# Prompt stick attention: f32r sums of a split softplus carried in PSUM, bias and mask added by TensorE, two query chains interleaved, limit and rounding on GpSimd

## What is computed

```python
def stick_breaking(q, k, v, q_pos, k_pos, bias):
    z = jnp.einsum('bqhd,bkhd->bhqk', q, k).astype(jnp.float32) * (q.shape[-1] ** -0.5)
    z = z + bias.astype(jnp.float32)[None, :, None, None]
    mask = k_pos[None, :] < q_pos[:, None]
    log_beta = jax.nn.log_sigmoid(z)
    log_keep = jnp.where(mask, jax.nn.log_sigmoid(-z), 0.0)
    suffix = lax.cumsum(log_keep, axis=3, reverse=True)
    after = jnp.concatenate([suffix[..., 1:], jnp.zeros_like(suffix[..., :1])], axis=-1)
    att = jnp.where(mask, jnp.exp(log_beta + after), 0.0)
    return jnp.einsum('bhqk,bkhd->bqhd', att.astype(v.dtype), v)
```

## Time and profile before

| | |
|---|---|
| median of 3 runs | 1787.25 us (1784.97 to 1789.44) |
| profiled execution, its own time | 1785.31 us |
| its span | 1783.5 us |
| TensorE busy in the span | 1488.5 us, 83% |
| VectorE, ScalarE, GpSimd busy | 649.3, 502.0, 170.1 us |
| prompt stick attention | from 344.6 to 460.5 us of the span, 115.9 us |

### The profile page before, as it was taken

How to read it: one execution, slowest core, us unless ns; L and a number is a source line. 1 busy time by engine, 2 the same in 40 slices (tenths; PEclk the granted TensorE clock), 3 DMA queues, 4 the chain that set the end, 5 groups by cost and what they waited for, 6 DMA issues and landing times. The chain is left out here.

```text
span 1783.5 us, 24367 instructions
## 1 busy us (share of the span) xinstructions
PE 1488.5 (83%) x9557; PEld 1034.4 (58%) x9558; DVE 649.3 (36%) x1011; ACT 502.0 (28%) x1050; POOL 170.1 (10%) x162
## 2 busy tenths in 40 slices
PE   5998997799857888698789989699639999999910
PEld 2446997555636777486349967478324444544400
DVE  4325352387212344567011023275341111111158
ACT  1114233387354343311011134221101111111122
POOL 0000000034102311000000000000011000000046
PEclk9998999699757999899889999899859999999965
DMA  8111110220003000300521044210546776622154
GB/s 296 53 53 30 47 48 24 65 65 1 1 2 111 14 3 3 120 1 1 214 92 48 2 188 166 108 42 1 232 171 226 304 301 229 234 94 94 71 190 148
DMA packets 78750, 182.59 MB, mean 102 GB/s; under 512 B 12692, under 2 KB 40475, under 8 KB 72243
## 3 DMA queue, kind: packets, MB, share of 16 engines
q1 hardware_dynamic: 66891, 137.74, 21.7%
q0 software_dynamic: 7008, 25.43, 4.0%
q10 hardware_dynamic: 4752, 18.02, 2.5%
HBM read 146.40 MB, written 34.86 MB: 102 GB/s over the span
## 5 line engine op out<-in xcount | busy, mean ns | idle before, releaser
L2882 PE MATMUL bank<-arena,hT 128*128 x512 | 232.7, 598 | 2.2 <-DVE hT L2989 2.2
L2882 PEld LDWEIGHTS bank<-arena,hT 128*128 128x128 f32 x512 | 95.9, 192 | 110.9 <-issue 110.9
L2902 PE MATMUL bank<-arena,hT 128*128 x256 | 115.3, 593 | 1.6 <-ACT hT L2940 1.6
L463 PE MATMUL bank<-arena,hT 128*128 128x512 f32 x256 | 112.8, 599 | 0.0
L2016 PE MATMUL bank<-hT_rest,f_w_high 128*128 128x352 f32 x288 | 93.4, 324 | 0.0
L2985 DVE TENSOR_TENSOR hT<-bank,hT 128x256 f32<-128x256 f32 x32 | 13.6, 425 | 216.8 <-ACT hT L2946 216.8
L2852 POOL DMA_INDIRECT hT<-tokens,row_token x32 | 34.2, 1067 | 603.4 <-PE bank L2868 307.2
L463 PEld LDWEIGHTS bank<-arena,hT 128*128 128x128 f32 x256 | 48.7, 193 | 58.4 <-issue 58.3
L2902 PEld LDWEIGHTS bank<-arena,hT 128*128 128x128 f32 x256 | 46.3, 191 | 48.2 <-issue 48.2
L2015 PE MATMUL bank<-hT_high,q_w_high 128*128 128x352 f32 x192 | 62.7, 327 | 7.8 <-DVE q_w_low L2335 7.8
L2015 PE MATMUL bank<-f_h_high_a,f_w_high 128*128 128x352 f32 x180 | 59.0, 328 | 6.7 <-DVE f_w_low L673 6.7
(11 more groups left out here) (463 smaller groups left out, 2955.6 us busy)
## 6 DMA issues: line engine op xcount, KB each, us to landing
arena<-in_ex_wg_dram SPq DMA_DIRECT2D x16, 1024.0 KB, 5.9
arena<-in_ex_wu_dram SPq DMA_DIRECT2D x16, 1024.0 KB, 8.8
arena<-in_ex_wd_dram SPq DMA_DIRECT2D x16, 1024.0 KB, 10.8
expert_rows<-hT ACTq DMA_DIRECT2D x32, 512.0 KB, 2.7
arena<-in_cache_mem_k_dram SPq DMA_DIRECT2D x8, 1024.0 KB, 4.9
arena<-in_w_in_dram SPq DMA_DIRECT2D x12, 512.0 KB, 4.0
h<-in_x_prompt_dram SPq DMA_DIRECT2D x8, 512.0 KB, 8.7
arena<-in_w_in_dram SPq DMA_DIRECT2D x2, 2048.0 KB, 16.7
```

The lines of the kernel that those rows point to most:

```text
L463: last = nc.tensor.matmul(ps[bank][0:r, 0:n], hT[:, k, i * P:i * P + r], wt[:, k, col:col + n], start=(k == 0), stop=(k == KC - 1))
L2882: last = nc.tensor.matmul(ps[UPB[u % 2]][:, :], xT[:, u % 2, k, :], gate_up_of[:, bass.ds(slot, 1), :, k, :].rearrange("p a g f -> p (a g) ...
L2902: last = nc.tensor.matmul(ps[DNB[q]][:, :], hidT[:, u % 2, f, :], down_of[:, bass.ds(slot, 1), f, q * 512:(q + 1) * 512].rearrange("p a n ...
```

## The change

All of it is in `stage_stick_prompt`.

- **Order.** The steps come from two chains of 18, query blocks 7, 4, 3, 0 and 6, 5, 2, 1, one step of either in turn. `first(n)` is a diagonal step, `final(n)` the last key block of a query block.
- **Bias and mask.** The bias is built once as an f32r tile (its rounded part in some rows, the rest of it in others, set by `sel`), and TensorE adds it to the scores by two f32r products with a matrix of ones; on the diagonal two more products add -1e30 where a key is hidden. ScalarE copies the finished scores from PSUM (`evacuate`).
- **Softplus.** GpSimd limits z to 30 (`cut`), ScalarE takes Exp and Ln(1 + x), VectorE the maximum with z. GpSimd rounds the result to f32r (`round_up`), VectorE forms the remainder, also f32r.
- **Sums.** A suffix is two f32r products, the triangle times the rounded part and times the remainder. The sum of earlier blocks stays in the PSUM bank of the chain: once the argument has been read, `rest` adds the other triangle (without the diagonal) times both parts, so that the bank holds the whole blocks.
- Rings grow: five `zb`, three `t`, three each of rounded parts and remainders. Four constant matrices are copied to f32r by ScalarE at the start, and the mask by VectorE.

The diff, cut to its core:

```diff
+    chains = [[(qb, kb) for qb in x for kb in range(qb, -1, -1)] for x in ((7, 4, 3, 0), (6, 5, 2, 1))]
+    steps = [x for two in zip(*chains) for x in two]
+    first = lambda n: steps[n][0] == steps[n][1]
+    final = lambda n: steps[n][1] == 0
+    carried = lambda n: sum(not final(m) for m in range(n + 1))
...
         @block.gpsimd
+            def cut(n):
+                pool.wait_ge(zb_ok, n + 1)
+                if n >= 3:
+                    pool.wait_ge(low_ok, n - 2)
+                nc.gpsimd.tensor_scalar(tmp[:, n % 3], zb[:, n % 5], 30.0, None, ALU.min).then_inc(cut_ok, 1)
+
+            def round_up(n):
+                pool.wait_ge(sp_ok, n + 1)
+                if n >= 3:
+                    pool.wait_ge(sums, n - 2)
+                    pool.wait_ge(carry, carried(n - 3))
+                nc.gpsimd.tensor_copy(high4[:, n % 3], tmp[:, n % 3]).then_inc(high_ok, 1)
+
+            for n in range(N + 2):
+                if n < N:
+                    cut(n)
+                if n >= 2:
+                    round_up(n - 2)
...
         @block.tensor
             def scores(n):
...
+                if n == 0:
+                    pe.wait_ge(consts_ok, 6)
+                    pe.wait_ge(bias_ok, 1)
+                for half in range(2):
+                    q = slice(half * DH, (half + 1) * DH)
+                    last = nc.tensor.matmul(ps[2 * (n % 2) + half][:, 0:256], one[q, :], bias[q, half * 256:(half + 1) * 256],
+                                            start=False, stop=not first(n), skip_group_check=True)
+                if first(n):
+                    for half in range(2):
+                        last = nc.tensor.matmul(ps[2 * (n % 2) + half][:, 0:256], eye, hide,
+                                                start=False, stop=True, skip_group_check=True)
                 last.then_inc(score, 1)
 
             def suffix(n):
                 if n >= 2:
                     pe.wait_ge(arg_ok, n - 1)
+                pe.wait_ge(high_ok, n + 1)
+                nc.tensor.matmul(ps[4 + n % 2][:, :], negsuf, high[:, n % 3 * W:(n % 3 + 1) * W],
+                                 start=first(n), stop=False, skip_group_check=True)
+                pe.wait_ge(low_ok, n + 1)
+                nc.tensor.matmul(ps[4 + n % 2][:, :], negsuf, low[:, n % 3 * W:(n % 3 + 1) * W],
+                                 start=False, stop=True, skip_group_check=True).then_inc(sums, 1)
+
+            def rest(n):
+                if final(n):
+                    return
+                pe.wait_ge(arg_ok, n + 1)
+                nc.tensor.matmul(ps[4 + n % 2][:, :], negbef, high[:, n % 3 * W:(n % 3 + 1) * W],
+                                 start=False, stop=False, skip_group_check=True)
+                nc.tensor.matmul(ps[4 + n % 2][:, :], negbef, low[:, n % 3 * W:(n % 3 + 1) * W],
+                                 start=False, stop=True, skip_group_check=True).then_inc(carry, 1)
...
+            for n in range(N + 5):
+                if n < N:
+                    scores(n)
+                if n >= 5:
+                    values(n - 5)
+                if 4 <= n < N + 4:
+                    rest(n - 4)
+                if 2 <= n < N + 2:
+                    suffix(n - 2)
...
         @block.scalar
+            def evacuate(n):
+                act.wait_ge(score, n + 1)
+                if n >= 5:
+                    act.wait_ge(exp_ok, n - 4)
+                nc.scalar.copy(by_pair(zb[:, n % 5]), score_banks(n)).then_inc(zb_ok, 1)
 
             def softplus(n):
+                act.wait_ge(cut_ok, n + 1)
+                t = tmp[:, n % 3]
+                link(nc.scalar.activation(t, t, ACT.Exp))
                 nc.scalar.activation(t, t, ACT.Ln, bias=1.0).then_inc(soft, 1)
...
+            for n in range(N + 4):
                 if n < N:
+                    evacuate(n)
+                if 1 <= n <= N:
+                    softplus(n - 1)
+                if n >= 4:
+                    weights(n - 4)
...
         @block.vector
+            link(nc.vector.tensor_copy(hi, z0))
+            link(nc.vector.tensor_tensor(z1, z0, hi.bitcast(F32), ALU.subtract))
+            link(nc.vector.tensor_scalar(z0, hi.bitcast(F32), sel[:, 0:1], None, ALU.mult))
+            nc.vector.scalar_tensor_tensor(bias4, z1, sel[:, 1:2], z0, ALU.mult, ALU.add).then_inc(bias_ok, 1)
 
             def soft_sum(n):
                 dve.wait_ge(soft, n + 1)
+                nc.vector.tensor_tensor(tmp[:, n % 3], zb[:, n % 5], tmp[:, n % 3], ALU.max).then_inc(sp_ok, 1)
+
+            def remainder(n):
+                dve.wait_ge(sp_ok, n + 1)
+                dve.wait_ge(high_ok, n + 1)
                 if n >= 3:
                     dve.wait_ge(sums, n - 2)
+                    dve.wait_ge(carry, carried(n - 3))
+                nc.vector.tensor_tensor(low4[:, n % 3], tmp[:, n % 3], high4[:, n % 3].bitcast(F32), ALU.subtract).then_inc(low_ok, 1)
 
             def argument(n):
                 dve.wait_ge(sums, n + 1)
+                nc.vector.tensor_tensor(zb[:, n % 5], head4(4 + n % 2), zb[:, n % 5], ALU.add).then_inc(arg_ok, 1)
...
             for n in range(N + 4):
+                if n < N:
+                    soft_sum(n)
+                if 2 <= n < N + 2:
+                    argument(n - 2)
+                if n < N:
+                    remainder(n)
+                if n >= 4 and final(n - 4):
+                    outputs(n - 4)
```

More of the change, by code:

```diff
@@ L890, in stage_stick_prompt @@
     nc, K = c.nc, c.K
[L891 to L899, removed]
+    W = HEADS * P
+    c.place(start=c.after_q, zb=5 * W, t=3 * W, high=3 * W, low=3 * W, att=2 * W, negsuf=P, negbef=P, eye=P, one=P,
+            bias=W, hide=2 * P)
@@ new lines, in ring @@
+    def ring(x, n):
+        return x.rearrange("p (s h q) -> p s h q", s=n, h=HEADS)
+    zb, tmp, att = ring(c.A("zb"), 5), ring(c.A("t"), 3), ring(c.A("att"), 2)
+    high, low = c.rounded("a_high", "high"), c.rounded("a_low", "low")
+    high4, low4 = ring(high, 3), ring(low, 3)
+    negsuf, negbef, eye, one, bias, hide = (c.rounded(f"a_{k}", k) for k in ("negsuf", "negbef", "eye", "one", "bias", "hide"))
+    sb, sel, bias4 = c.new_small(HEADS), c.new_small(2), bias.rearrange("p (h q) -> p h q", h=HEADS)
@@ L908, in stage_stick_prompt @@
+    sums, carry, arg_ok, exp_ok, pv, out_ok = s("a_sums"), s("a_carry"), s("a_arg"), s("a_exp"), s("a_pv"), s("a_out")
     dve_chain, act_chain = s("a_dve"), s("a_act")
-    last_of = [max(n for n, x in enumerate(steps) if x[0] == qb) for qb in range(NT)]
     def head4(bank):
@@ L961, in scores @@
                         q = slice(half * DH, (half + 1) * DH)
-                        last = nc.tensor.matmul(ps[2 * (n % 2) + half][:, pair * P:(pair + 1) * P],
-                                                kT[q, pair, kb * P:(kb + 1) * P], qT[q, pair, qb * P:(qb + 1) * P],
-                                                start=True, stop=True)
+                        nc.tensor.matmul(ps[2 * (n % 2) + half][:, pair * P:(pair + 1) * P],
+                                         kT[q, pair, kb * P:(kb + 1) * P], qT[q, pair, qb * P:(qb + 1) * P],
+                                         start=(pair == 0), stop=False, skip_group_check=True)
@@ L981, in values @@
             def values(n):
                 qb, kb = steps[n]
[L983 to L988, removed]
+                pe.wait_ge(exp_ok, n + 1)
+                if first(n):
+                    before = [m for m in ends if m < n and m % 2 == n % 2]
+                    if before:
+                        pe.wait_ge(out_ok, ends.index(before[-1]) + 1)
@@ L991, in values @@
                         hd = 2 * pair + half
-                        last = nc.tensor.matmul(ps[6 + qb % 2][half * DH:(half + 1) * DH, pair * P:(pair + 1) * P],
+                        last = nc.tensor.matmul(ps[6 + n % 2][half * DH:(half + 1) * DH, pair * P:(pair + 1) * P],
                                                 vtok[:, kb, hd * DH:(hd + 1) * DH], att[:, n % 2, hd, :],
-                                                start=(kb == qb and pair == 0), stop=(kb == 0), skip_group_check=True)
+                                                start=(first(n) and pair == 0), stop=(kb == 0), skip_group_check=True)
                 last.then_inc(pv, 1)
[L997 to L1005, removed]
+            for n in range(N + 5):
[7 more added lines that the diff above has]
+                    suffix(n - 2)
         @block.scalar
@@ L1037, in _ @@
+            hi = high4[:, 2]
             for h in range(HEADS):
[L1038 to L1047, removed]
+                nc.vector.tensor_scalar(z0[:, h % 2 * 2 + h // 2, :], K("ones"), sb[:, h:h + 1], None, ALU.mult).then_inc(bias_set, 1)
```

86 lines of the change are left out of this document (21 added, 65 removed).

## The result

The changed kernel takes 1883.85 us (median of 4 runs, 1880.0 to 1889.56) against 1786.11 for the kernel before in runs beside it: ratio 1.0548 (95% interval 1.0512 to 1.0583), 5.5% slower. The profiled execution took 1880.0 us, 94.7 more than that of before. The next stage begins at 556.22 us where it began at 460.52, so the whole loss, 95.7 us by these starts, comes from the stage.

A forecast was written before the change was run, and what follows sets the result against it. The prediction took a ring through the engines' queues as the bound, 4.20 us per lap; 38.5 + 3 + 4.2 + 3 gave +49 us on the stage, so 1836 us on the median's footing, range 1816 to 1872.

The forecast's parts named there:

- The ring: In prompt stick attention, waits in program order through four engines' queues close a loop paid every step: 4.20 us per lap.
- Its five members: Second suffix product waits for remainder, scores behind it, evacuation for scores, limit for evacuation with rounding behind, remainder for rounding.
- (c): Rival: the ring has slack, the busiest engine counts at 2.5 us per step, kernel faster at 1779 us; chance 0.08.
- (d): Rival: products named f32r run as f32, the waiting product takes 0.96 for 0.34 us, +20, 1856 us; chance 0.02.
- the price of the limit: GpSimd's limit in the lap, priced like its one-input copy at 0.61 us, upper end 1.275 us.
- the new lap lies nearer to the first: TensorE, busy about 2.8 of 4.2 us, resembles an earlier stretch busy 1.27 of 2 us that kept full clock.
- 3 us for a start at half clock: TensorE begins the stage at half clock, about 1.0 us more per lap, taken for three laps.
- no engine over 70: Sign that the forecast is right: no engine over 70% busy in the stage.
- 0.50 in the middle: Sign that the forecast is wrong: a granted clock of 0.5 in the middle of the stage.
- rival (a): TensorE's clock stays low: 1865 us if low throughout, in between if it changes back and forth; chance 0.15.
- (b): Rival: GpSimd's passes cost as with two inputs; one slow +21, 1857 us, both 1879 us; chance 0.13.
- 3 + 4.2 = 7.2: Before the first argument: about 3 us of dependent bias passes, and 4.2 us because argument(0) stands behind remainder(1).

The follow-up runs named there:

- run 4: Changed kernel with a plain GpSimd copy in place of the limit (limit left out): 1840.35 us, ratio 1.0296 to the kernel before.
- run 6: Changed kernel with eight extra zero-matrix products per turn keeping TensorE busy: 1863.14 us, ratio 1.0424 to the kernel before.
- run 1: Changed kernel with GpSimd's rounding put ahead of its limit, no instruction changed: 1793.86 us, ratio 1.0038 to the kernel before.
- run 8: Changed kernel with rounding ahead of the limit, scores a turn earlier and a GpSimd copy for the limit: 1783.07 us, ratio 0.9960 to the kernel before.
- run 9: Changed kernel with the limit moved to VectorE two steps ahead, GpSimd only rounding, scores a turn earlier: 1776.71 us, ratio 0.9946 to the kernel before.

## Why the prediction was right in kind and short by half

**Right.** The ring exists and sets the step. Its five members stand in the groups above as listed, and undoing either of two of its edges without touching an instruction removes 71 to 90 us. TensorE leaves its bound, VectorE waits ahead of each remainder, the evacuation is released by TensorE and the limit by the evacuation. The rivals that a slack ring gives a faster kernel (c) and that f32r runs as f32 (d) fall: every f32r product is one record, 36 on line 998. The other terms of the lap come out near at full clock, together 0.18 shorter. Product to scores was 0.43 (0.34 forecast), scores to bias 0.47 (0.65), bias to evacuation 0.40 (0.49 with the hand-over), evacuation 0.67 as forecast. With a 0.61 us pass for the limit, run 4 measured 3.97 us per full-clock lap against 4.15, 4.17 per step against 4.20, and a stage 48.8 us later against +49; part of that agreement is a shorter lap offset by a clock that was not full throughout.

**Wrong: the price of the limit.** "Both new passes read one tensor, so I take 0.61 each; 1.275 each is the upper end." The rounding is 0.611; the limit is 1.487, above the end. I priced a pass by its number of tensors, and by the nearest row that shared this number, a plain copy. At full clock this term is 1.00 of the lap (4.97 against 3.97), some 34 us over the stage (35 x 0.98, by the 4.95 of run 6). An addition with two tensors is no ceiling for a pass with one and a number. By the Trainium skill, GPSIMD Engine Reference, section Engine selection, a pass with one input runs at roughly line rate; the trace agrees for the rounding and the copy at 0.61 us and not for the limit at 1.487 us, and the measurement decides.

**Wrong: the clock.** The step "the new lap lies nearer to the first", on the earlier trace rows, and 3 us for a start at half clock. TensorE was busy for 152.86 of the stage's 211.40 us, 72% where the prediction wanted no engine over 70, and its clock fell and rose all through: the 0.50 in the middle that the prediction had named as a sign against it. Run 6 prices that at 18 us, so 15 more than forecast. I had weighed rival (a) as low throughout, with the middle case in half a sentence. The two misses add to each other: the longer pass leaves TensorE more idle time, and with the copy (run 4) most of the clock's share went too: 145.8 us from first to last remainder are 7 above 35 full-clock laps of 3.97.

**The sum.** 34 for the limit, 15 for the clock, less 6 for a lap that was otherwise 0.18 shorter, make 43. The first argument came 12.3 us late where 3 + 4.2 = 7.2 was forecast besides the 3 for the clock, which stands in the 15: 5 more. Of these, 1.7 lie in the lap that this term holds (the first two remainders start at 359.83 and 365.71, 5.88 us apart in place of 4.2); the rest I did not trace. Together that is 48 against the nearly 47 by which 95.7 exceeds 49, and the terms come from different runs. The range held (a) and one slow pass of (b), each at its price alone and the pass at 1.275: both together at their measured prices lie outside it.

## What to carry to other kernels

When a step is spread over several engines, write down for each queue what stands behind each wait, and follow it until it meets itself: a ring that advances the index by one is paid in full every step, however idle the engines are, and reordering two lines of a loop can be worth more than halving a pass. Look at once for the next ring, through the buffers, since cutting one uncovers it. Price a pass by a row of its own instruction form on its own engine; where there is none, let the range go well beyond the nearest form, and count that an engine left waiting may lose its clock too.

## What the runs showed of the hardware that was not expected

- GpSimd's pass of 128x512 f32 with a tensor and a number takes 1.487 us, as minimum or as multiplication; its copy and its rounding take 0.61, its addition of two tensors 1.275. VectorE does the same minimum in 0.41 to 0.44 where no pass of GpSimd has just begun.
- VectorE's remainder, with two inputs in SBUF, takes 0.69 us alone, 1.15 started together with GpSimd's limit and 1.01 started 0.14 us after its copy; the limit grows from 1.49 to 1.71 or 1.79 where VectorE's passes were there first. In the changed kernel itself the ring keeps the two apart, so none of its loss is this. The Trainium skill, SBUF — State Buffer, section SBUF: two separate sides, describes a shared pair of ports that is held for a whole instruction while the other engine is blocked. The trace agrees that the two engines hinder one another, but not on a full block: the remainder from 402.00 to 403.15 in run 1 ends before the limit that began at 401.99 and lasted 1.49 us. In all these rows VectorE's pass ends as if it had begun about 0.47 us after GpSimd's, an estimate from start offset plus stretch: 0.01 + 0.46 beside the limit (run 1), 0.14 + 0.32 beside the copy (run 8), 0.15 + 0.32 and 0.26 + 0.20 beside the rounding (run 9, against 0.43). So in these rows the start of GpSimd's pass counts and not its length, and a pass of VectorE that starts 0.46 us after it (402.26 in run 9) or 1.08 us after it (403.07 in run 1) keeps its time.
- Extra products that compute nothing made a kernel 21 us faster, by keeping the granted clock at 1.00 where it had alternated between 1.2 and 2.4 GHz.
